# State-space steps: the state's contribution and the skip term summed in the scores' PSUM bank, the weighted rows in a buffer of their own

## The reference, cut to what matters

```
decay  = exp(where(mask, cum_i - cum_j, -inf))
y_diag = einsum(scores * decay, x*dt)                      # within the chunk
states = einsum(B, decay_end, x*dt)                        # what the chunk adds to the state
y_off  = einsum(C, state before the chunk, exp(cum))       # what the state adds to the chunk
y = y_forward + y_backward + x * d_skip
y = rms_norm(y * silu(z), ssd_norm)
```

## Time and profile before

| | us |
|---|---|
| median of 3 executions | 1039.81 (1035.92 to 1043.4) |
| the profiled execution | 1041.73 |
| its span, first to last instruction | 1040.1 |
| PE busy / DVE busy / ACT busy / POOL busy | 886.0 / 338.8 / 269.2 / 85.1 |
| mean granted clock of TensorE over the span | 0.92 |

### The profile page before, as it was taken

How to read it: one execution, slowest core, us unless ns; L and a number is a source line. 1 busy time by engine, 2 the same in 40 slices (tenths; PEclk the granted TensorE clock), 3 DMA queues, 4 the chain that set the end, 5 groups by cost and what they waited for, 6 DMA issues and landing times.

```text
span 1040.1 us, 13662 instructions
## 1 busy us (share of the span) xinstructions
PE 886.0 (85%) x5573; PEld 469.1 (45%) x5573; DVE 338.8 (33%) x827; ACT 269.2 (26%) x644; POOL 85.1 (8%) x96
## 2 busy tenths in 40 slices
PE   3899999677787999849989959997998948989985
PEld 0455656355344655433233318654555533332325
DVE  0423415665466511321011015454552140210112
ACT  2313313324254500321021023214551141210110
POOL 2400001011100000230000020000000150000002
PEclk8899999888898999859999989997999958999996
DMA  9999999966775011355999967033001244999915
GB/s 380 428 428 379 365 373 387 378 220 250 280 270 221 2 61 60 122 234 196 421 415 415 423 263 303 1 121 132 2 1 39 88 177 186 403 428 421 426 80 182
DMA packets 36336, 258.96 MB, mean 249 GB/s; under 512 B 3408, under 2 KB 3552, under 8 KB 21424
## 3 DMA queue, kind: packets, MB, share of 16 engines
q1 hardware_dynamic: 20448, 198.27, 47.2%
q0 software_dynamic: 12224, 47.01, 12.3%
q10 hardware_dynamic: 3600, 12.78, 3.1%
HBM read 236.73 MB, written 54.87 MB: 280 GB/s over the span
## 4 chain that ended last, share of the span: by engine, by line
PE 75%; DVE 8%; DMA 7%; ACT 5%; issue 3%; POOL 2%; POOLq 0%; SPq 0%; DVEq 0%; ACTq 0%
PE ps L520 21%; PE ps L687 14%; PE ps L709 8%; PE ps L951 6%; PE ps L534 3%; DMA U<-expert_rows 3%; PE ps L481 3%; PE ps L671 3%; PE ps L763 3%; PE ps L541 2%; DMA xT<-x_in 2%; PE ps L565 2%; ACT hT L1089 1%; DMA expert_rows<-U 1%; DVE hT L1774 1%
## 5 line engine op out<-in xcount | busy, mean ns | idle before, releaser
L687 PE MATMUL ps<-ring,U 128*32 128x512 f32 x1200 | 166.3, 592 | 0.0
L520 PE MATMUL ps<-U,ring 128*128 128x384 f32 x320 | 106.4, 489 | 3.8 <-DVE U L1522 2.5
L687 PEld LDWEIGHTS ps<-ring,U 128*32 128x32 f32 x1200 | 47.5, 110 | 85.3 <-issue 85.0
L709 PE MATMUL ps<-ring,U 128*32 128x512 f32 x672 | 85.7, 594 | 0.0
L520 PEld LDWEIGHTS ps<-U,ring 128*128 128x128 f32 x320 | 59.6, 189 | 48.0 <-issue 5.0
L687 PE MATMUL ps<-hT,U 128*32 128x512 f32 x168 | 73.1, 592 | 0.0
L687 PE MATMUL ps<-U 128*32 128x512 f32 x168 | 73.1, 592 | 0.0
L481 PE MATMUL ps<-ring,cond_w 128*32 128x384 f32 x512 | 56.5, 573 | 16.9 <-DVE misc L1693 8.8
L671 PE MATMUL ps<-small,U 128*128 128x128 f32 x192 | 31.9, 319 | 38.1 <-DMA U<-expert_rows 36.0
L951 PE MATMUL ps<-ring,hT 128*128 128x384 f32 x192 | 63.2, 488 | 1.1 <-issue 0.9
L520 PE MATMUL ps<-hT,ring 128*128 128x384 f32 x192 | 63.3, 488 | 0.9 <-issue 0.8
(11 more groups left out here) (296 smaller groups left out, 1221.6 us busy)
## 6 DMA issues: line engine op xcount, KB each, us to landing
ring<-w_in SPq DMA_DIRECT2D x102, 1536.0 KB, 11.2
expert_rows<-w_in POOLq DMA_DIRECT2D x16, 2048.0 KB, 91.3
U<-expert_rows SPq DMA_DIRECT2D x24, 512.0 KB, 6.2
expert_rows<-U ACTq DMA_DIRECT2D x24, 512.0 KB, 9.5
hT<-w_in SPq DMA_DIRECT2D x6, 1536.0 KB, 12.3
U<-w_in SPq DMA_DIRECT2D x6, 1536.0 KB, 15.6
small<-small_in SPq DMA_DIRECT2D x1, 3147.5 KB, 37.7
xT<-x_in SPq DMA_DIRECT2D x1, 1536.0 KB, 16.8
```

What stands on the lines that cost most here:

```text
L520: ins = mm(out, lhs(k), rhs(k), start=(k == 0), stop=(k == n - 1))
L687: ins = mm(ps[q:q + 32, r, :], xgT[:, r, P * k + q:P * k + q + 32], w[e][:, c:c + 512], start=(k == 0), stop=(k == DC - 1))
L709: ins = mm(ps[q:q + 32, 6 + h, :], actT_of[i % NR][:, P * j + q:P * j + q + 32], w[e][:, c:c + 512], start=(j == 0), stop=(j == 1))
```

## The change

- The four products of the state (`off`, before L894) go to the head of a step, between the transposes of `turn_step`; DVE multiplies them by exp(cum) at once, into four SBUF buffers `off_in`. PE then adds these buffers into banks 5 and 6 by products with the identity (`add_off`), between the first `cums` groups.
- x times `d_skip` is computed by POOL (`dx_ready`), and PE adds it into banks 5 and 6, again by two products with the identity. POOL's queue holds it ahead of the step's four additions of directions.
- DVE's tail is one product: banks 5 and 6 times the gate.
- The weighted rows have a buffer of their own (`weighted`, `xw_of`), so DVE writes the first ones right after the gate product, PE makes the first new state before it turns y, and DVE no longer waits for the turning. In step 3 the second state follows behind the "end" modulation product.
- The list `jobs` and PE's waits follow this order. Two semaphores are merged (`e_in` into `dt_ready`).

The diff's core:

```diff
-        xw = ytok = oTm[:, 0:1024]
-        ytmp = oTm[:, 1024:1536]
+        ytok = oTm[:, 0:1024]
+        OFFS = [(1, 0), (1, 1), (0, 0), (0, 1)]
+        off_in = dict(zip(OFFS, (oTm[:, 1024:1536], dec[4], dec[5], dec[3])))
+        tile0 = oTy3[:, :, 0:P]
+        def weighted(i, half=None):
+            x = zs3[:, 1, :].rearrange("p (c n) -> p c n", c=8) if i > 1 else tile0
+            return x if half is None else x[:, 4 * half:4 * half + 4, :]
...
+            def off(i, n):
...
+                d, g = OFFS[n]
+                if n == 0:
+                    pe.wait_ge(S["st_done"], 1)
+                if n == 2:
+                    pe.wait_ge(S["st_done"], 1 if t == 1 else 2)
+                b = fill("off", i, d, g)
+                filled(mm(b[:, 0:512], xc3[64 * g:64 * g + 64, 9, c0:c0 + P], s_in[64 * g:64 * g + 64, :], start=True, stop=True))
+            def add_off(i, n):
...
+                pe.wait_ge(S["free_dve"], emptied[index[("off", i, d, g)]][1])
+                mm(ps[:, 5 + g, :], ident, off_in[d, g], start=(n < 2), stop=True, skip_group_check=True)
...
                     cums(0)
                     cums(1)
+                    add_off(i, 0)
+                    add_off(i, 1)
                     late_ada("unit", i, -1)
                     cums(2)
+                    add_off(i, 2)
+                    add_off(i, 3)
                     cums(3)
+                    pe.wait_ge(S["dx_ready"], nfull + 1)
+                    for g in range(2):
+                        mm(ps[:, 5 + g, :], ident, weighted(i, g), start=(t == 0), stop=True, skip_group_check=True)
...
-                    if t:
-                        for d in range(2):
...
                     late_ada("tail", i)
+                    for d in STATES[i][:1]:
+                        state(i, d)
                     pe.wait_ge(S["ynormed"], nfull + 1)
...
-                for d in STATES[i]:
+                for d in STATES[i][1:]:
                     state(i, d)
...
+                if full:
+                    if t:
+                        for d, g in OFFS:
+                            b = take("off", i, d, g)
+                            emptied_by(tt(cut(off_in[d, g], 8), cut(b[:, 0:512], 8), spread(e96[5][...], PS), MUL))
...
                     dve.wait_ge(S["diag_done"], 4 * nfull + 4)
-                    link(tt(cut(ytok, HS), cut(xtok, HS), spread(sm("d_skip"), PS), MUL))
-                    link(tt(ytok, ytok, ps[:, 5:7, :].rearrange("p a n -> p (a n)"), ADD))
...
-                    tt(ytok, ytok, zs3[:, t, :], MUL).then_inc(S["ysq_ready"], 1)
+                    tt(ytok, ps[:, 5:7, :].rearrange("p a n -> p (a n)"), zs3[:, t, :], MUL).then_inc(S["ysq_ready"], 1)
+                    for d in STATES[i][:1]:
+                        weight_rows(d)
+                    if len(STATES[i]) < 2:
+                        dve.sem_inc(S["xtok_used"], 1)
                     dve.wait_ge(S["ynorm_ready"], nfull + 1)
                     link(dve.reciprocal(ssd_r, ssd_r))
                     ts(ytok, ytok, ssd_r[:, 0:1], None, MUL).then_inc(S["ynormed"], 1)
-                    after("yT", i, 1)
+                    for d in STATES[i][:1]:
+                        new_state(d)
+                    for d in STATES[i][1:]:
+                        weight_rows(d)
+                        new_state(d)
...
             for n in range(NT * 4):
+                if n % 4 == 0:
+                    i = n // 4 + 1
+                    pool.wait_ge(S["xtok_ready"], i + 1)
+                    if i == 1:
+                        pool.wait_ge(S["st_done"], 1)
+                    else:
+                        pool.wait_ge(S["ynorm_ready"], i - 1)
+                    pool.tensor_tensor(by_half(weighted(i)), by_chunk(xtok), over_heads(sm("d_skip")), MUL).then_inc(S["dx_ready"], 1)
```

More of the change, by code:

```diff
@@ L143, in build @@
         dec = [hTt[:, 512 * i:512 * i + 512] for i in range(4)] + [oTm[:, 512 * i:512 * i + 512] for i in range(2)]
-        xw = ytok = oTm[:, 0:1024]
-        ytmp = oTm[:, 1024:1536]
+        ytok = oTm[:, 0:1024]
[5 more added lines that the diff above has]
+            return x if half is None else x[:, 4 * half:4 * half + 4, :]
+        xw_of = lambda i: [oTm[:, 512 * g:512 * g + 512] if i == 0 else weighted(i, g) for g in range(2)]
+        by_chunk = lambda ap: ap.rearrange("p (c a n) -> p c a n", c=8, a=2)
+        by_half = lambda ap: ap.rearrange("p c (a n) -> p c a n", a=2)
+        over_heads = lambda ap: ap.rearrange("p (c a) -> p c a", a=2).unsqueeze(3).broadcast_to([P, 8, 2, PS])
         s_b1, Gs, Btok = region(TAIL, 512, 256, 128)
@@ L290, in build @@
                         continue
[L291 to L298, removed]
-                        if t:
-                            for d in range(2):
[L301 to L304, removed]
-                    for d in STATES[i]:
+                    for n, name in enumerate([("xt", i, 0), ("xt", i, 1), ("bt", i), ("g", i, 0), ("g", i, 1)]):
+                        if t and n < 4:
+                            job(("off", i) + OFFS[n], "D")
+                        job(name, "A")
+                    for u in range(8):
+                        job(("bc", i, u), "D")
+                    for d in STATES[i][:1]:
+                        job(("st", i, d), "D")
+                    job(("yT", i, 0), "A")
+                    job(("yT", i, 1), "A")
+                    for d in STATES[i][1:]:
                         job(("st", i, d), "D")
@@ L794, in turn_step @@
                 for k in range(2):
+                    off(i, k)
                     b = fill("xt", i, k)
@@ L798, in turn_step @@
                     filled(ins)
+                off(i, 2)
                 b = fill("bt", i)
@@ L855, in _ @@
                 if full:
+                    off(i, 3)
                     for g in range(2):
@@ L1763, in _, with weight_rows, new_state @@
                     modulation(1)
-                dve.wait_ge(S["xtok_ready"], i + 1)
                 col = lambda d: slice(48 * d + HS * t, 48 * d + HS * t + HS)
+                def weight_rows(d):
+                    link(tt(by_half(weighted(i)) if i else by_chunk(oTm[:, 0:1024]), by_chunk(xtok if i else xtok0), over_heads(e96[7][:, col(d)]), MUL))
+                    dve.sem_inc(S["xw_ready"], 1)
+                def new_state(d):
+                    b = take("st", i, d)
+                    for g in range(2):
+                        r = slice(64 * g, 64 * g + 64)
+                        dst = {(2, 1): s_b1, (1, 0): h0[0], (0, 0): h0[0], (0, 1): h0[1]}[t, d]
+                        if t == 0:
+                            ins = dve.tensor_copy(dst[r, :], b[r, :])
+                        else:
+                            cd = e96[8][r, 48 * d + HS * t + 8 * g:48 * d + HS * t + 8 * g + 8]
+                            link(tt(cut(dst[r, :], 8), cut(h0[d][r, :], 8), spread(cd, PS), MUL))
+                            ins = tt(dst[r, :], dst[r, :], b[r, :], ADD)
+                        link(ins)
+                    dve.sem_inc(S["free_dve"], 1)
+                    dve.sem_inc(S["st_done"], 1)
+                if not full:
+                    dve.wait_ge(S["xtok_ready"], i + 1)
+                    weight_rows(1)
+                    new_state(1)
+                    dve.sem_inc(S["xtok_used"], 1)
                 if full:
+                    if t:
+                        for d, g in OFFS:
+                            b = take("off", i, d, g)
+                            emptied_by(tt(cut(off_in[d, g], 8), cut(b[:, 0:512], 8), spread(e96[5][:, 48 * d + HS * t + 8 * g:48 * d + HS * t + 8 * g + 8], PS), MUL))
                     def segment(u):
@@ L1807, in _ @@
                     ts(ytok, ytok, ssd_r[:, 0:1], None, MUL).then_inc(S["ynormed"], 1)
-                    after("yT", i, 1)
-                    nfull += 1
[L1810 to L1826, removed]
+                    for d in STATES[i][:1]:
+                        new_state(d)
+                    for d in STATES[i][1:]:
+                        weight_rows(d)
+                        new_state(d)
+                    nfull += 1
             rot = lambda n, t, w: sm(n)[:, w * (t - 1):w * t]
```

38 lines of the change are left out of this document (16 added, 22 removed).

## The result

The changed kernel took 1029.41 us (median of 4, 1025.26 to 1031.36) where the kernel before, run beside it, took 1040.3 (median of 4, 1035.92 to 1043.4): a ratio of 0.9893 with the interval 0.9845 to 0.9941. That is 10.9 us, faster by 1.07%, just beyond the 1% that can be told from no change. The profiled execution took 1030.51 (before 1041.73), and its span is 1028.9. PE is busy 895.1 us (before 886.0), DVE 326.4 (338.8), POOL 91.2 (85.1).

The account below looks back on a forecast made before the run. It took a chain of waits to bound the stage: PE inside steps, one engine at a time between. Seven pieces summed to -16.3 us, so 1041.73 gives 1025.4 profiled, median 1023.5; own range 1017 to 1029, 8 in 10 1016.5 to 1033.

Parts of the forecast that it names:

- head of step 1: From the first head to step 1's first decay groups: four `off` products added, +3.8 us.
- inside step 1: From first decay groups to last scores' products: six identity products added, 23.3 us against 20.1, +3.2.
- tail 1 and head 2: Between steps 1 and 2: shorter DVE tail, y in time for PE, 11.8 us against 21.3, -9.5.
- inside step 2: From step 2's first decay groups to its last scores' products: 23.3 us against 21.9, +1.4.
- tail 2 and head 3: Between steps 2 and 3: ACT's row copy and table load decide, 13.0 us against 20.2, -7.2.
- inside step 3: From step 3's first decay groups to its last scores' products: two identity products, no cover taken, +1.9 us.
- tail 3: From step 3's last scores' products to the MLA products: 7.7 us against 17.6, -9.9.
- Rival 3: POOL's skip product late for PE: all gain lost at 13.4 us, about 1054 us at 18; chance 0.05.
- rival 2: Gain given back behind the stage if ring weights come late: 1036 to 1041 us; chance 0.07.
- I keep 1.0 of wait: Inside step 1: 1.0 us of wait kept on PE's 22.3 us of products, bounds 0 and 3.5.
- the 3.5 us: Inside step 1 of before: 20.1 us less PE's 16.6, taken as waits for DVE and POOL and slow clock.
- Rival 1: Stage clock stays at mean 0.85: +15.7 us, gain 0.6, 1039 us; half of it 1031; chance 0.12.

Follow-up runs that it names:

- ada_first: The changed kernel with one modulation product of each step moved from behind the third group of `diag` to ahead of it: 1021.06 us, ratio 0.9820.
- fill_transposes: The changed kernel with twelve needless 128x128 transposes behind the second `diag` of each full step: 1023.17 us in one execution.
- buffer_alone: The kernel before with only the weighted rows' own buffer and the state ahead of turning y; sums stay in DVE's tail: 1025.07 us, ratio 0.9861.
- the repeats: The changed kernel and buffer_alone, with two other kernels, timed again side by side on one chip, six executions each: 1029.09 and 1025.21 us.
- ada_copy: ada_first with ACT's copy of the modulation row moved behind the root in step 2's tail: 1017.75 us, ratio 0.9795; repeated, 1016.75 us.

## Why the prediction was right, and where it was not

The direction held, and the median lies in the range, though 0.4 us above the upper end of the forecast's own (1029). That the range held it is in part luck: its upper end was drawn for identity products at the low clock, and these ran fast; the products that ran slow were others. The pieces by the prediction's own cuts, in us:

| piece | before | forecast | changed | ada_first |
|---|---|---|---|---|
| head of step 1 | 1.6 | 5.4 | 5.9 | 5.9 |
| inside step 1 | 20.1 | 23.3 | 24.2 | 22.1 |
| tail 1 and head 2 | 21.3 | 11.8 | 13.7 | 12.1 |
| inside step 2 | 21.9 | 23.3 | 24.3 | 22.1 |
| tail 2 and head 3 | 20.2 | 13.0 | 12.9 | 12.7 |
| inside step 3 | 18.5 | 20.4 | 20.8 | 18.7 |
| tail 3 | 17.6 | 7.7 | 9.5 | 7.8 |
| stage | 121.2 | 104.9 | 111.4 | 101.4 |

**What was priced right.** Apart from the slow pair in steps 1 and 3 (1.7 each) the tails shrank as forecast: DVE's gate product follows the last `diag` directly, ACT's square follows it 1.25 behind its start, PE makes the state ahead of the turning of y and in steps 1 and 3 y is there when PE gets to it. DVE's and ACT's timelines in step 1's tail:

```profile
189.75 1.23 DVE L1858 TENSOR_TENSOR U<-ps,U 128x1024 f32<-128x1024 f32 x1 [3.33 <-PE ps L904]
```

```profile
191.00 1.06 ACT L1311 ACTIVATE U<-U 128x1024 f32<-128x1024 f32 x1 [5.14 <-DVE U L1858]
```

Identity products took 0.86 each (estimate 0.945), a single `off` product up to 1.05 (0.945), the POOL product 1.90 (2.5), with 7.8, 7.8 and 3.0 us to spare before PE wants it. Rival 3 (POOL late) falls by this, and rival 2 (given back behind the stage) by the 758.0 us that are left behind the stage against 758.5.

**The step that failed** is a term of the sum, the price of the inside of a step, "I keep 1.0 of wait", together with the full-speed prices of the products behind it, 1.43, 1.10 and 2.86 "since the engine is now dense around them". The wait of a step did not go away and did not shrink to 1.0; one wait of 1.67 us stays ahead of the third `diag`, and the added products stand ahead of it, not in it. Its direct cost is small, but the clock falls behind it, and the slow products reach into the tail. That is about 8 us of slow products, of which 1.6 came back through smaller terms (fourteen identity products at 0.86 instead of 0.945 alone give 1.2). The prediction had named slow clock among the 3.5 us that it found inside step 1 of before, and then kept a price for the wait alone. Rival 1 had the right quantity, a clock short of 1.00 in a stage bound by PE (0.91 where it feared 0.85), and about half its price; it put it on the transposes and on PE as a whole, and fill_transposes and ada_first show the place to be the wait. The evidence lay in the trace of before, in PE's timeline at the same place, where only the mean of a ten-us stretch of another step had been read the earlier trace rows:

```profile
176.89 1.69 PE L871 MATMUL ps<-hT,U 128*128 128x64 f32 x8 [1.67 <-DVE U L1784]
178.52 2.52 PE L481 MATMUL ps<-ring,cond_w 128*32 128x384 f32 x16
```

The same wait, the same slow modulation product behind it. The last column of the table bears this out: with that wait filled, every piece but the head comes out at or under its forecast or within 0.3 of it, and the stage 3.5 under it.

**What the prediction took for one gain was two edits whose gains do not add up.** It credited the shorter tails to the whole change. buffer_alone shows that the buffer and the state's order alone win 13.4 us of the stage. With the sums PE is busy 102.1 us of the stage, without them 83.4, and in the order of the change this costs 3.9 us in the repeats. With the wait inside the step filled, the stage gains by the sums (101.4 against 104.6) and the medians don't show it; with ACT's copy moved too, the medians show 5.5, part of which may be the move's own.

**What stays open** is why the same 1.67 us lets the clock fall in all three steps of the changed kernel (in both of its profiles), but in the kernel before only in steps 1 and 2, and in buffer_alone only in step 1 (in both of its profiles). What PE did ahead of the wait differs, and so does the time at which it comes; no run here separates the two.

## What to carry to other kernels

Here, on top of the buffer, moving sums from a vector engine's tail to TensorE paid in the stage only once the wait behind them was filled. A short wait that is left behind the added products can cost more through the clock than by its own length (1.67 us, and 3.2 us of slow products behind it in steps 1 and 3), so look at the products behind each wait in the trace, not at the mean clock of a stretch. Put independent work of TensorE into such a wait; where none is at hand, even needless products can win. And time the parts of a change apart: here one of two halves alone was better than both.

## What the runs showed of the hardware that was not expected

- A wait of 1.67 us was followed by some 7 us at a granted clock of 0.50 with PE busy throughout (186 to 193 in the changed kernel); the three waits lasted 5.0 us in all, and the slow products behind them cost about 8 more. In step 3 of the kernel before and in steps 2 and 3 of buffer_alone the same wait was followed by fast products.
- Six needless products of 128x512 shortened the stage by 6.9 us, thirty-six needless transposes by 8.1 (one execution).
- In two profiles of one kernel (ada_copy) with the same busy time ahead, the clock fell in one and not in the other, and the stage differed by 3.2 us.
- POOL's product of 128x1024 with a repeated factor took 1.90 us, 1.5 times its addition of 128x512 (1.267), not twice.
